# Selected-attention layer: sixteen heads over blocks first, sixteen over the band second, with the second kind's keys and values as filling work

## The reference, cut to what matters

```
def nsa_attention(h, w_in, w_out, cmp_pos, cmp_w1, cmp_w2, rel_table):
    q, kc, vc, ks, vs, kw, vw, gate = split(h @ w_in)      # 16 query heads, 4 groups of keys and values
    kc_b = compress_kv(kc, cmp_pos[0], cmp_w1[0], cmp_w2[0])
    vc_b = compress_kv(vc, cmp_pos[1], cmp_w1[1], cmp_w2[1])
    p_cmp = masked_softmax(q @ kc_b * scale, cmp_end <= t)
    o_cmp = p_cmp @ vc_b
    o_slc = selected_block_attention(q, ks, vs, sel_idx, rel_table)
    o_win = banded_attention(q, kw, vw, rel_table, 512)
    g = sigmoid(gate)
    o = g[..., 0] * o_cmp + g[..., 1] * o_slc + g[..., 2] * o_win
    return o @ w_out
```

## Time and profile before

| what | value |
|---|---|
| median of three runs | 3314.49 us |
| the profiled execution's own time | 3317.67 us |
| its span, first to last instruction | 3315.9 us |
| PE busy | 3261.1 us (98%) |
| DVE busy | 2034.8 us (61%) |
| ACT busy | 1743.1 us (53%) |
| mean granted TensorE clock | 0.995 |
| HBM | 188 GB/s over the span |

### The profile page before, as it was taken

One profiled execution on the slowest core, in us unless ns is written; L12 is line 12 of the kernel. 1 busy time (PEld: TensorE's weight loads), 2 busy tenths in 40 slices (PEclk: granted clock), 3 DMA queues, 4 the chain that ended last, 5 costly groups with the idle time before them and its releaser, 6 DMA issues.

```text
span 3315.9 us, 53125 instructions
## 1 busy us (share of the span) xinstructions
PE 3261.1 (98%) x20062; PEld 2893.1 (87%) x20062; DVE 2034.8 (61%) x2777; ACT 1743.1 (53%) x2539; POOL 70.3 (2%) x150
## 2 busy tenths in 40 slices
PE   8999999999999999999999999999999999999999
PEld 7899988888999888888888889888888988888887
DVE  5567565555675656567656567655656665656755
ACT  4457544444674444446545457544445654545644
POOL 0000000000000000000000000000000000000000
PEclk9999999999999999999999999899999999999999
DMA  6666355455653554545545555255555455455454
GB/s 254 219 224 223 141 182 187 179 199 188 222 175 142 186 190 179 190 176 178 197 184 187 185 194 195 83 201 187 195 186 192 163 191 186 183 189 193 163 190 177
DMA packets 105598, 617.93 MB, mean 186 GB/s; under 512 B 10919, under 2 KB 19239, under 8 KB 35560
## 3 DMA queue, kind: packets, MB, share of 16 engines
q1 hardware_dynamic: 85576, 565.52, 46.6%
q10 hardware_dynamic: 19872, 50.34, 4.6%
HBM read 614.71 MB, written 9.50 MB: 188 GB/s over the span
## 4 chain that ended last, share of the span: by engine, by line
PE 91%; DVE 3%; ACT 2%; issue 1%; POOL 0%; ACTq 0%; DMA 0%; POOLq 0%; DVEq 0%; SPq 0%
PE ps L2075 24%; PE ps L2079 12%; PE ps L2210 7%; PE ps L2209 7%; PE ps L2211 7%; PE ps L2191 5%; PE ps L2193 5%; PE ps L2192 5%; PE ps L2150 4%; PE ps L2096 2%; PE ps L2097 2%; PE ps L2098 2%; DVE wlo L1326 1%; PE ps L2579 1%; ACT v L789 1%
## 5 line engine op out<-in xcount | busy, mean ns | idle before, releaser
L1326 DVE TENSOR_TENSOR wlo<-raw,whi 128x2048 fp32r<-128x2048 f32 x435 | 996.5, 2292 | 574.5 <-ACT whi L756 574.1
L2075 PE MATMUL ps<-xhl,whi 128*128 128x512 f32 x3456 | 1202.0, 397 | 0.0
L756 ACT CAST whi<-raw 128x2048 fp32r<-128x2048 f32 x435 | 828.0, 1903 | 145.2 <-PE ps L2211 110.5
L2079 PE MATMUL ps<-xhl,wlo 128*128 128x256 f32 x3456 | 893.6, 279 | 0.0
L2075 PEld LDWEIGHTS ps<-xhl,whi 128*128 128x128 f32 x3456 | 627.5, 188 | 121.6
L2079 PEld LDWEIGHTS ps<-xhl,wlo 128*128 128x128 f32 x3456 | 651.7, 189 | 37.4
L2210 PE MATMUL ps<-wlo,ht 128*128 128x512 f32 x1056 | 417.3, 395 | 0.0
L2209 PE MATMUL ps<-whi,ht 128*128 128x512 f32 x1056 | 417.2, 395 | 0.0
L2211 PE MATMUL ps<-whi,ht 128*128 128x512 f32 x1056 | 416.7, 395 | 0.0
L2191 PE MATMUL ps<-xhl,whi 128*128 128x256 f32 x1360 | 391.7, 288 | 2.4 <-DVE wlo L1326 2.4
L2193 PE MATMUL ps<-xhl,wlo 128*128 128x256 f32 x1360 | 385.8, 284 | 0.0
(11 more groups left out here) (318 smaller groups left out, 3857.5 us busy)
## 6 DMA issues: line engine op xcount, KB each, us to landing
raw<-stream SPq DMA_DIRECT2D x528, 1024.0 KB, 4.8
bias<-rel_bias ACTq DMA_DIRECT2D x80, 256.0 KB, 2.6
gain<-gains ACTq DMA_DIRECT2D x18, 1024.0 KB, 4.8
bias<-fixed_bias ACTq DMA_DIRECT2D x40, 256.0 KB, 2.8
rel_bias<-rel_vectors SPq DMA_DIRECT2D x16, 512.0 KB
x<-x_tokens SPq DMA_DIRECT2D x2, 512.0 KB, 6.5
gain<-gains SPq DMA_DIRECT2D x1, 512.0 KB, 7.9
y_tokens<-x SPq DMA_DIRECT2D x1, 512.0 KB, 2.6
```

The lines of the kernel that those rows point to most:

```text
L756: nc.scalar.copy(whi[:, slot, :], raw[:, slot, :]).then_inc(sem["hi_ready"], 1)
L1326: nc.vector.tensor_tensor(wlo[:, slot, :], raw[:, slot, :], whi[:, slot, :].bitcast(F32), ALU.subtract).then_inc(sem["lo_ready"], 1)
L2075: wide = lambda: pe.matmul(ps[:, bank, 0:2 * half], hi[:, k, col0:col0 + P], src[:, k0 + k, :], start=first and k == 0, stop=last and k == ...
L2079: e = pe.matmul(ps[:, bank, 0:half], lo[:, k, col0:col0 + P], src[:, k0 + k, 0:half], start=False, stop=False)
```

## The change

The 16 heads of kind 0 run first, then the 16 of kind 1. The query items move ahead (each is now needed four slots after the one before), and the second kind's keys (`k` 4) and values (`v` 256) move behind the compression and are filling work of slots 9 to 10 and 16 to 17. The tables of slots, turns and the numbers `NSA_GELU`, `NSA_PROBS`, `NSA_ADD` are new. All compressed parts are now added into an `o` that holds something, so the copy on DVE becomes an addition. `blocks_made(0)` hangs on the end of `cmp` 1 and `blocks_made(1)` on the end of `q` 8.

```diff
     items = [one("v", 0, 4, "act"), one("q", 0, 5, "dve"), one("k", 0, 6, "dve"), Item("gate", 0, 1, (7,), 2, "act"),
-             Item("gate_turn", 0, 0, (7,), 1, "dve"), one("cmp", 0, 4, "act"), one("cmp", 1, 5, "act"), one("k", 4, 6, "dve"), one("v", 256, 7, "act"),
-             one("q", 4, 4, "dve"), Item("hidden", 0, 2, (5, 6), 4, "dve"), one("q", 8, 7, "dve"),
...
+             Item("gate_turn", 0, 0, (7,), 1, "dve"), one("q", 4, 4, "dve"), one("cmp", 0, 5, "act"), one("cmp", 1, 6, "act"),
+             one("q", 8, 7, "dve"), Item("hidden", 0, 2, (4, 5), 4, "dve"), Item("hidden", 1, 2, (6, 7), 4, "dve"),
+             one("q", 12, 4, "dve"), one("k", 4, 6, "dve"), Item("blocks", 0, 0, (5,), 1, "act"),
+             Item("cmp_scores", 0, 0, (7,), 8, "dve"), one("v", 256, 4, "act"), Item("cmp_turn", 0, 0, (5, 6), 1, "act"),
...
-                     [5, 4, 4, 2, 2, 4, 2, 2, 2, 2, 2, 1, 2, 1, 1, 1, 1, 4, 4, 0, 0, 0, 1, 2, 0, 0, 0, 2, 2, 2, 1, 2, 1, 1, 0])
-NSA_TURNS = {25: 0, 26: 1, 27: 2, 28: 3, 29: 4, 30: 5, 32: 6, 34: 7}
-NSA_GELU = 14
-NSA_PROBS = 19
-NSA_ADD = 24
+                     [5, 4, 4, 3, 3, 3, 3, 2, 1, 2, 3, 1, 3, 0, 3, 2, 2, 2, 1, 1, 1, 0, 0, 0, 0, 1, 1, 1, 0, 1, 2, 2, 1, 1, 1])
+NSA_TURNS = {22: 0, 23: 1, 24: 2, 26: 3, 28: 4, 30: 5, 32: 6, 34: 7}
+NSA_GELU = 8
+NSA_PROBS = 16
+NSA_ADD = 21
...
-    group, kind, i = t // 8, t % 8 // 4, t % 4
+    kind, group, i = t // HEADS, t % HEADS // 4, t % 4
...
-    return 8 * (k // 2) + 4 + 2 * (k % 2) + 2
+    return HEADS + 2 * k + 2
...
-                            if 8 * g + 4 < NSA_ADD:
-                                e = nc.vector.tensor_tensor(to, made, to, ALU.add)
-                            else:
-                                e = nc.vector.tensor_copy(to, made)
-                            e.then_inc(sem["cmp_added"], 1)
+                            nc.vector.tensor_tensor(to, made, to, ALU.add).then_inc(sem["cmp_added"], 1)
...
-                    elif (item.kind, item.at) == ("k", 4):
+                    elif (item.kind, item.at) == ("cmp", 1):
                         blocks_made(0)
-                    elif (item.kind, item.at) == ("v", 256):
+                    elif (item.kind, item.at) == ("q", 8):
                         blocks_made(1)
...
-                    add = kind == 1 or t + 2 >= NSA_ADD
+                    add = kind == 1
```

More of the change, by code:

```diff
@@ L241, in nsa_items @@
     items = [one("v", 0, 4, "act"), one("q", 0, 5, "dve"), one("k", 0, 6, "dve"), Item("gate", 0, 1, (7,), 2, "act"),
-             Item("gate_turn", 0, 0, (7,), 1, "dve"), one("cmp", 0, 4, "act"), one("cmp", 1, 5, "act"), one("k", 4, 6, "dve"), one("v", 256, 7, "act"),
-             one("q", 4, 4, "dve"), Item("hidden", 0, 2, (5, 6), 4, "dve"), one("q", 8, 7, "dve"),
-             Item("hidden", 1, 2, (4, 5), 4, "dve"), one("q", 12, 6, "dve"), Item("blocks", 0, 0, (4,), 1, "act"),
-             Item("cmp_scores", 0, 0, (7,), 8, "dve"), Item("cmp_turn", 0, 0, (5, 6), 1, "act"), Item("cmp_values", 0, 0, (7, 4), 1, "add"),
-             Item("cmp_values", 1, 0, (5, 6), 1, "add")]
+             Item("gate_turn", 0, 0, (7,), 1, "dve"), one("q", 4, 4, "dve"), one("cmp", 0, 5, "act"), one("cmp", 1, 6, "act"),
+             one("q", 8, 7, "dve"), Item("hidden", 0, 2, (4, 5), 4, "dve"), Item("hidden", 1, 2, (6, 7), 4, "dve"),
+             one("q", 12, 4, "dve"), one("k", 4, 6, "dve"), Item("blocks", 0, 0, (5,), 1, "act"),
+             Item("cmp_scores", 0, 0, (7,), 8, "dve"), one("v", 256, 4, "act"), Item("cmp_turn", 0, 0, (5, 6), 1, "act"),
+             Item("cmp_values", 0, 0, (7, 4), 1, "add"), Item("cmp_values", 1, 0, (5, 6), 1, "add")]
     items += [Item("out", i, 1, (), 4, "") for i in range(4)]
```

## The result

The changed kernel took 3330.86 us (median of 6 runs, 3327.75 to 3341.39), the kernel before 3314.61 us (6 runs, 3312.61 to 3319.43; the three given further up are among them). The ratio is 1.0048 with an interval of 1.0036 to 1.0060: slower, by 12 to 20 us, which is 0.4 to 0.6%. The forecast was 3319 with a range up to 3328, so the direction was the forecast's and the size was outside its range.

The account below looks back on a forecast made before the run. PE, busy 98% of the span, was taken to bound the kernel, so reordering changes only waits and low clock. Terms -3.9 + 12.1 + 0 - 1.4 - 2.1 = +4.7 us on the 3314.5 median gave 3319, range 3309 to 3328.

Parts of the forecast that it names:

- A: Slots 3 and 4: the wait for k 4 goes, since it is made well before its use; -3.9 us.
- B: Slots 3 to 7: new waits on DVE, 8.7 us, plus low clock, 3.4 us; +12.1, between +8.7 and +13.8.
- C: Slots 8 to 17: about as much lost as in the kernel before; 0, between -1 and +2 us.
- D: Slots 18 to 29: loss 12.3 us against 13.7, with a 5.0 us wait before the turn; -1.4, between -5 and +3.
- E: The end: out2.2 covers the wait after the last turn, and low clock may stay out; -1.3 and -0.8 us.
- B's low-clock term: Slots 3 to 7: two stretches of 3.4 us at low clock, each up to 1.7 us of matmul time; +3.4 us.
- Rival 2: The clock falls after every new wait, three stretches each in slots 5 to 8 and 18 to 25: +9.6, 3324 us; chance 0.25.
- Rival 1: DVE's queue is not late in slot 5, hidden1.0 finds its input ready: -6.0, 3308.5 us; chance 0.15.
- rival 3: Waits only change places, the k 4 wait becoming one for the block input alone: 0 +- 2 us; chance 0.10.

Follow-up runs that it names:

- filled waits: Changed kernel with 13, 31, 12 and 17 unread 256-column matmuls in the four waits of slots 5 to 7: 3321.49 us, ratio 1.0016.
- the end's cover: Kernel before with only out2.2 moved from slot 33 to slot 34, behind the last turn: 3313.19 us, ratio 0.9995.
- the wide and the narrow stall: Kernel before with extra DVE additions: 10 in slot 7, wait ahead of q8 (wide), 3319.40 us; 14 in slot 9, wait among hidden1 parts (narrow), 3326.02 us.
- both tables together: Changed kernel with filling of slots 3 to 17 spread evenly and the turn of the compressed probabilities one slot later: 3323.11 us, ratio 1.0023.
- the first experiment: Changed kernel with only the filling of slots 3 to 17 spread evenly, gelu two slots later: 3331.04 us, ratio 1.0053.
- items apart and filled waits: Changed kernel with q 12 between the hidden items, probabilities a slot earlier, k 4 in bank 6, unread wide matmuls in five waits: 3305.17 us, ratio 0.9969.

## Why the prediction was wrong

By its own steps, in us:

| step | forecast | measured | from |
|---|---|---|---|
| A, wait for k 4 | -3.9 | -3.9 | the loss of before; no wait at head 4 or 16 after |
| B, waits of slots 3 to 7 | +8.7 | +9.8 at most at full clock, 5.3 as they stand | filled waits; windows |
| B, low clock there | +3.4 | +9.0 net, 13.5 of matmul time | the same |
| C, slots 8 to 17 | 0 | 0 | 38.99 for 37.1 of work, about as much lost as before |
| D, slots 18 to 29 | -1.4 | -0.5 | 41.49, 28.3 of work |
| E, the end | -2.1 | -2.6 | 24.05, two parts more than before |
| sum | +4.7 | +11.8 | phase +12.2 |

This table is against the profiled execution of the kernel before, as the forecast was.

*A was right*, and what became of it too: `q` items are early enough and `k4` is two slots clear.

*B's waits were right in place and cause.* The late inputs are the low pieces (`wlo`, line 1339) before `hidden0.2` and `q12.0`, and `blocks_made(1)` (`blk`, line 1897) before `hidden1.0`. The first and the last of the three took 1.44 and 2.06 us against 1.6 and 2.1 forecast. The one for the block input took 1.77 against 3.7, since PE, at half speed from 2018.5 on, came to it 20.7 us after the start of slot 3 and not 18.2. For the same reason the wait of 1.4 before `hidden1.2` did not come: its pieces were ready. Timeline of DVE in slot 5 of the kernel after, from `biased` to the end of `blocks_made(1)`:

```profile
2015.29 0.29 DVE L1973 CUSTOM_DVE_ANT_0 s<-ps,bias 128x128 f32<-128x128 f32 x1
...
2015.85 2.96 DVE L1339 TENSOR_TENSOR wlo<-raw,whi 128x512 fp32r<-128x512 f32 x3
2018.84 1.39 DVE L1877 TENSOR_TENSOR q<-ps,q 64x512 fp32r<-64x512 f32 x2
2020.26 1.99 DVE L1891 TENSOR_TENSOR cblk<-cmp_source,prm 128x240 f32<-128x240 f32 x4
...
2022.98 1.16 DVE L1897 TENSOR_TENSOR blk<-cblk,blk 128x960 fp32r<-128x960 f32 x1
```

From 2015.29 to 2024.14 these are 8.85 us in a row without a gap, as the forecast's rows added up (0.65, 0.60 and two of 1.14, 1.42, 3.80: 8.75).

*The step that failed is B's low-clock term*: "between none and three stretches of 3.4 us, each up to 1.7 us of matmul time. I take two". I took the length of a stretch from row 1 of rows 7, where 256-column matmuls follow the wait, and carried it to a place where `hidden` parts of 120 and 60 columns follow. There it was one stretch of 30.9 us, which cost 9.0 us net where +3.4 stood in the sum. Slots 3 to 7 took 49.03 us where the forecast had 39 to 44. The forecast did name this as what would make it wrong ("if the low clock took more than 7 us in either place"), but the price was not in its range: with all three stretches the term was 5.1 us. The second row of rows 7, 10.20 us behind slots without filling, was the hint that a stretch can last; I used it for a rival's "for" and not for the length.

*Rival 2* (the clock falls after every new wait, 3324) had the mechanism, but counted three stretches of 3.4 us in slots 5 to 8 where there was one through all of them. Rival 1 did not happen: it wanted `blocks_made(1)` at 18.2 us from PE's start of slot 3, and it ended at 22.2 (2024.14 less 2001.90), where the forecast had 21.8. Nor did rival 3, since the pieces' waits did not vanish.

*C was sized right, D's waits too.* The wait before the turn was forecast at 5.0 and is 4.92, the one before the first turn 2.1 and 1.97; slots 18 to 29 took 41.49 us, inside the 38 to 43. The `out` part at the end has no wait.

*The losses of before that D and E started from were partly chance.* The forecast took them from one execution, whose time of 3317.67 us was 3.2 over the median, took that difference to be the same for both kernels, and added its sum to the median. Three other traces have slots 18 to 29 of the kernel before untouched (the end's cover, the wide and the narrow stall): 45.12, 45.31 and 46.83 us against 48.33, so 10.5 to 12.2 us lost and not 13.7. The two stalls have its end untouched too: 22.15 against 23.72. Against the lowest of these D is +2.7 and not -0.5, and E, the two added parts taken out, -1.0 and not -2.6. The sum then is -3.9 + 9.8 + 9.0 + 0 + 2.7 - 1.0 = +16.6, an estimate from single traces, and the medians differ by 16.2. So against the medians the forecast missed by some 12 us: about 6 by the low-clock term, 1 by the waits of B, 5 by D and E. That D and E look right in the table is in part luck.

A reading was off as well, without consequence: the wait ahead of head 4, "2.4 us" in the forecast, is 2.17.

The Trainium skill ("TensorE: Matmul & The Clock Gate", Why this matters for your kernels) advises against long PE idle gaps between bursts of matmuls. Here short gaps were enough: 0.58, 1.06, 1.44 and 1.49 us had the low clock behind them. The same page (Part 1) has PE back at the full rate after sustained matmuls. The runs agree where wide matmuls follow (4.34 us) and disagree where narrow ones do (19.95 us busy without a gap, at 0.50).

*What remains open.* The medians differ by 16.2 us and the profiled executions by 11.2; only the latter has a trace. The kernel's runs differ by 13.6 us among themselves with mean clocks of 0.990 to 0.993, so the slow stretches are probably longer or more in others, but that is argued and not shown; 3.1 of the 5.0 us between the two differences come from the kernel before, whose profiled execution was that much over its median. Nor is it shown why a wait of 0.58 us ahead of `cmp_scores` brings the low clock in some executions and not in others: with the same table for these slots, it fell in slot 14 with both tables together and stayed at 1.00 with spread filling alone, and the kernel after kept 1.00 in slot 12. And in the profiled run of the first experiment the phase took 167.2 us, while its other runs took 8 to 12 us more. Last, no run changed the width of one and the same matmul. The `hidden` and `cmp_scores` matmuls differ from those of a projection in their operands too, and every matmul has a weight load of its own (20062 of each on the page), so a narrow one has more loading per column. That it is the width that matters is argued; shown is that these matmuls ran on at 0.50 and the 256-column ones did not.

## What to carry to other kernels

Price a wait of PE by what PE does behind it. Ahead of 256-column matmuls a wait of 1.48 us cost only itself here, and one of 3.03 us 5.3 us in all; ahead of a long row of narrow ones 2.68 us of waiting cost 11.9, and a busy share of 100% hid it. Compare with more than one trace of the kernel before, since a low stretch that comes and goes there moves what a change seems to win. When reordering, put wide work behind the waits that cannot be avoided and keep the narrow work for where PE comes running; where neither is possible, some useless wide matmuls inside the wait are worth their code. In a profile, look for windows whose busy time equals their length and whose granted clock is 0.50.

## What the runs showed of the hardware that I had not expected

- The granted clock stayed at 0.50 over 19.95 us of matmuls without a gap (120 and 60 columns, with one 256-column part in them), and over 18.60 us in the kernel after. Yet the same matmuls ran at 1.00 where no wait stood ahead of them: a slot with two `hidden` parts does so in the kernel before, and this is the kernel with items apart and filled waits, slot 9:

```profile
2030.48:2035.50 5.02, 5.02 (x47) 1.00 0.50 144
```

- Matmuls that do nothing useful made the kernel quicker: 59 wide ones in five waits, 3318.35 to 3305.17 us.
- Waits of about the same length (1.49 and 1.48 us, the same releaser) had the clock at 0.50 or at 1.00 behind them, by what followed. The fall came not in the wait but 1.9 us later, among narrow matmuls, and so it was behind the one of 1.44 us.
